# A pooling branch folded into the output projection of a one-core encoder block

## The chip, the cores and the metric

The kernel runs on one core of one Trainium2 chip. The metric is device time in microseconds, the median of several runs. Engines are called by their names here: TensorE (PE in rows) multiplies matrices, VectorE (DVE), ScalarE (ACT) and GpSimd (POOL) work element by element, and SyncE (SP) issues most of the DMA transfers; ScalarE issues some of them too.

## What is computed

One layer of an encoder on 2048 tokens of width 1024, in float32:

```python
h = rms_norm(x, norm1_g)
q, k, v, p = split(h @ w_in)                    # 512, 128, 128, 512 columns
a = sliding_window_sink_attention(rms_norm(q), rms_norm(k), v, sinks)
# pooling, four groups g of 128 channels, windows w = 2, 4, 8, 16
mixed = trailing_mean(p[g], w) - p[g]
m[g]  = (mixed @ pool_w[g] + pool_b[g]) * pool_scale[g]
x = x + concat([a, m]) @ w_out                  # w_out is 1024 x 1024
x = x + conv_glu(rms_norm(x, norm2_g), w_up, conv_w, conv_b, w_down)
```

The pooling map is linear and is followed by a linear projection. So `m @ w_out[512:]` is `mixed` times the product of `pool_w`, the scale and the lower half of `w_out`, plus a constant row that depends on `pool_b`.

## The kernel before

Each float32 operand of TensorE is split in a high and a low half (type fp32r in the rows), and each product is three passes (`passes`, lines 808 to 812: high by high, low by high, high by low). ScalarE makes the high half of a weight tile (`w_hi`), VectorE the low half (`w_lo`), from rows that a DMA brings to one of two `raw` slots. The ring of split weights has three slots, and a unit's halves are made when the unit two places ahead of it is reached (`split(n + LEAD)`).

The tokens go in four blocks a = 0 to 3 of 512. A block has "units", each with one weight tile of 128x1024: four `pin` (p of a pooling group), two `kv`, four `q` and eight `o` (the output projection; the name o(a, h, k) holds the half h of the columns and k of the rows of `w_out`). A unit has 24 products of 128x512, about the same for kv in 48 of 128x256. Units of block 0 are split and their halves are stored to `wA_d` in DRAM, so that later blocks only load them; o units are split anew each time.

What happens when is written out by hand in `attention_order`. Each engine walks that one list and does its own part of every entry, in that order, waiting on semaphores. An engine that waits lets all that stands behind it wait too. These entries matter here:

- `win(a, g)`: VectorE forms the trailing mean less the token in `pbuf`, and then `mix_hi` and `mix_lo` from it.
- `pm(a, g)`: TensorE multiplies these by `pool_w[g]` (`pw_hi`, `pw_lo`), ScalarE evicts with scale and bias (line 1181) into `pbuf`. 16 of them in all.
- `join(a)`: VectorE splits that result into the lower rows of `cat_hi`, `cat_lo`, the left operand of the o units.
- `q(a, 3)`, the last q unit: ScalarE squares each tile (line 1209), VectorE sums (line 1621), GpSimd takes the reciprocal root (lines 2041 and 2043), VectorE scales (line 1626). VectorE does this inside its entry for q(a, 3), so its next weight split, that for o(a-1, 0, 2), stands behind the last scaling.
- `n1sq`, `n1sc`: the squares, roots and scaling of the rows of the next block. `n2sq`, `n2sc`: the same for the second norm. The roots are GpSimd's.
- `inv(a, j)`: GpSimd scales the softmax rows (line 2076).
- `o(a, h, 3)`: VectorE adds the product to the residual rows, `rows[a]`, which a DMA brought from x (line 1615).
- `t2(a, j)`: TensorE transposes the normed rows of block a (line 1033).

Blocks overlap: the o units of block a-1 come after the q units of block a. After the attention part come the up-projection with the convolution and the down-projection (`up`, `load_t`, `load_s`), which the diff does not touch.

Of the kernel before, what the change touches and what calls it, by code (L numbers as in the profile page):

```python
# [5 lines left out]
ALU = mybir.AluOpType  # L6
# [26 lines left out]
RAW, RING, LEAD, MIX = 2, 3, 2, 2  # L33


def attention_order():
# [13 lines left out]
    for a in range(NB):  # L50
        more, back = a + 1 < NB, a > 0
        if a > 1:
            units("kv", a, (0,))
            units("t2", a - 2, (2,))
            units("kv", a, (1,))
            units("kve", a, ())
            units("t2", a - 2, (3,))
        units("q", a, (0,))
        units("pm", a, (0,), (1,))
# [3 lines left out]
        units("q", a, (1,))  # L63
        units("win", a, (3,))
# [3 lines left out]
        units("pm", a, (2,))  # L68
        units("q", a, (3,))
        if back:  # L70
            units("pm", a, (3,))
        else:

            units("t1", a + 1, (0,))
            units("pm", a, (3,))
# [44 lines left out]
        units("inv", a, (1,))  # L120
        if more:
# [49 lines left out]
UNIT_STAGES = ("pin", "kv", "q", "o")  # L171
# [8 lines left out]
SPLIT_NO = {}  # L180
for _n, _s in enumerate(UNITS):
    if _s[1] == 0 or _s[0] == "o":
        SPLIT_NO[_n] = len(SPLIT_NO)
N_SPLIT = len(SPLIT_NO)
KEPT_UNITS = [n for n in SPLIT_NO if UNITS[n][0] != "o"]
# [52 lines left out]
def pm_bank(a, g):  # L238

    return (4, 5, 4, 5 if a == 0 else 7)[g]  # L240
# [84 lines left out]
def bass_hybrid_block(nc, x, norm1_g, w_in, q_norm_g, k_norm_g, attn_sinks, pool_w, pool_b, pool_scale,  # L325
# [15 lines left out]

    with ExitStack() as ctx:
# [32 lines left out]
        def at(name, kib, shape, dt=F32):  # L375
# [8 lines left out]
        mix_hi, mix_lo = at("mix_hi", 68.125, [P, MIX, T], F32R), at("mix_lo", 72.125, [P, MIX, T], F32R)  # L384
        pw_hi, pw_lo = at("pw_hi", 76.125, [P, 4, P], F32R), at("pw_lo", 78.125, [P, 4, P], F32R)
        raw = at("raw", 80.125, [P, RAW, 1024])
# [48 lines left out]
            "mix_ready pool_done m_copied mT_step mT_ready kv_done k_squared k_summed k_step k_rstd k_scaled v_kept "  # L435
# [25 lines left out]
        VECTORS_IN, CONST_IN, CONST_POOL, CONST_STEP, CONST_READY = 7 * 16, 6 * 16, 9, 5, 4  # L461
# [131 lines left out]
        def _(sp):  # L593
            def load(n, src):
                if n in SPLIT_NO:
                    m = SPLIT_NO[n]
                    wait(sp, "split_lo", m - RAW + 1)
                    sp.dma_start(raw[:, m % RAW, :].rearrange("p (k n) -> p k n", k=src.shape[1]), src
                                 ).then_inc(raw_in[m % RAW], 16)
# [27 lines left out]
            def kv(a, n, k):  # L627
# [3 lines left out]
                if k == 1 and a == 1:  # L631
                    sp.wait_ge(S["mix_ready"], 4)
                    sp.wait_ge(const_ready, CONST_READY)
                    sp.dma_start(r[:], x_v[:, 0:NT, :]).then_inc(r_in[0], 16)
# [81 lines left out]
            walk(dict(pin=pin, kv=kv, q=q, o=o, first_loads=first_loads, second_loads=second_loads))  # L716
# [91 lines left out]
        def _(pe):  # L808
# [73 lines left out]
            def pin(a, n, g):  # L882
                halves_there(n)
                if a == 1 and g < 2:

                    pe.wait_ge(S["m_copied"], 3 + g)
# [18 lines left out]
            def pm(a, g):  # L905
                if a == 0 and g == 0:
                    pe.wait_ge(const_ready, CONST_READY)
                pe.wait_ge(S["mix_ready"], 4 * a + g + 1)
                if g < 2:

                    pe.wait_ge(S["p_copied"], 4 * a + g + 1)
                    wait(pe, "h2_copied", KT * (a - 1))
                else:
                    pe.wait_ge(S["m_copied"], 4 * a + g - 1)
                    if pm_bank(a, g) == 7:
                        pe.wait_ge(S["k_scaled"], 2 * a + 2)
                passes(ps[:, pm_bank(a, g), :], pw_hi[:, g, :], pw_lo[:, g, :], mix_hi[:, g % MIX, :],
# [1243 lines left out]
```

## Time and profile before

| | us |
|---|---|
| median of 3 runs | 1776.51 |
| lowest and highest | 1775.22, 1776.84 |
| span of the profiled execution, first to last instruction | 1774.4 |
| TensorE busy | 1755.5 |
| VectorE busy | 1334.7 |
| ScalarE busy | 805.7 |
| GpSimd busy | 247.3 |

No time of the profiled execution apart from its span is given; the span lies 2.1 us under the median of the runs, which also counts what comes ahead of and behind the instructions. Busy time is what the engine spent in instructions; products overlap, so busy TensorE says that it always had one in its pipe. A row of the timeline gives the start, the duration, the engine and line, what was written from what, how many alike are merged (x4), and in brackets the idle time ahead and who ended it.

### The profile page before, as it was taken

What the parts mean: (1) busy time and instruction counts of PE and PEld (TensorE: products, weight loads), DVE (VectorE), ACT (ScalarE), POOL (GpSimd) and SP (SyncE); (2) the same over time, 40 slices, a digit from 0 to 9 for tenths busy, and PEclk for the clock granted to TensorE, in tenths of its full rate; (3) what the DMA queues carried; (4) which work ended last, traced back from release to release, by engine and by line L of the source; (5) the groups of instructions that cost most, each with busy time, mean ns of one, the idle gap of its engine ahead of it and who ended that gap; (6) DMA issues with size and microseconds to landing.
All of it is one profiled execution on the core that took longest, in us unless ns stands there. A gap on an engine that the chain in (4) does not pass through costs nothing.

```text
span 1774.4 us, 23434 instructions
## 1 busy us (share of the span) xinstructions
PE 1755.5 (99%) x8490; PEld 1462.7 (82%) x8490; DVE 1334.7 (75%) x1796; ACT 805.7 (45%) x1437; POOL 247.3 (14%) x270
## 2 busy tenths in 40 slices
PE   7999999999999999999999999999999999999999
PEld 6888888888878888888888888888888888888887
DVE  5645644635779999999998998998998778865774
ACT  4554544534765444444454444444444433333321
POOL 1213212202110000000000000000004033310210
PEclk9999999999999999999999999999999999999999
DMA  8553383484445523323376223223227999976884
GB/s 324 225 220 107 114 311 110 166 290 160 164 171 186 194 84 128 133 83 95 119 251 211 72 83 96 71 84 95 72 83 235 343 343 332 314 254 211 302 286 130
DMA packets 211555, 321.73 MB, mean 181 GB/s; under 512 B 13737, under 2 KB 106097, under 8 KB 211441
## 3 DMA queue, kind: packets, MB, share of 16 engines
q1 hardware_dynamic: 192014, 267.75, 45.3%
q10 hardware_dynamic: 19427, 52.49, 7.6%
q8 instruction: 68, 1.11, 0.3%
q14 instruction: 46, 0.38, 0.1%
HBM read 249.93 MB, written 70.25 MB: 180 GB/s over the span
## 4 chain that ended last, share of the span: by engine, by line
PE 92%; DVE 3%; DMA 2%; ACT 2%; issue 1%; POOL 0%; ACTq 0%; DVEq 0%; POOLq 0%
PE ps L810 29%; PE ps L811 29%; PE ps L812 29%; PE ps L969 1%; PE ps L993 1%; PE ps L980 1%; PE ps L1033 1%; DMA raw<-in_w_out_dram 1%; DMA raw<-in_w_in_dram 1%; DMA gT_d<-cb 0%; DVE hT_lo L1564 0%; DVE va_lo L1788 0%; DVE w_lo L1517 0%; POOL ss_q L2043 0%; PE ps L956 0%
## 5 line engine op out<-in xcount | busy, mean ns | idle before, releaser
L810 PE MATMUL ps<-va_hi,wv 128*128 128x512 f32 x1232 | 479.8, 389 | 1.4 <-DVE va_lo L1751 0.6
L811 PE MATMUL ps<-va_lo,wv 128*128 128x512 f32 x1232 | 479.3, 389 | 0.0
L812 PE MATMUL ps<-va_hi,wv 128*128 128x512 f32 x1232 | 479.3, 389 | 0.0
L810 PEld LDWEIGHTS ps<-va_hi,wv 128*128 128x128 f32 x1232 | 231.3, 188 | 51.3 <-issue 2.8
L812 PEld LDWEIGHTS ps<-va_hi,wv 128*128 128x128 f32 x1232 | 231.3, 188 | 48.0
L811 PEld LDWEIGHTS ps<-va_lo,wv 128*128 128x128 f32 x1232 | 231.3, 188 | 47.6
L810 PE MATMUL ps<-dt_hi,ds_hi 128*128 128x512 f32 x616 | 239.6, 389 | 0.0
L812 PE MATMUL ps<-dt_hi,ds_lo 128*128 128x512 f32 x616 | 239.6, 389 | 0.0
L811 PE MATMUL ps<-dt_lo,ds_hi 128*128 128x512 f32 x616 | 239.6, 389 | 0.0
L1838 DVE SCALAR_TENSOR_TENSOR cb<-ub,cst,cb 128x1024 f32<-128x1024 f32 x176 | 219.8, 1291 | 10.1 <-ACT cb L1357 10.1
L1357 ACT ACTIVATE cb<-ub,cst 128x1024 f32<-128x1024 f32 x88 | 108.9, 1243 | 142.7 <-DVE ub L1893 86.3
L1471 ACT ACTIVATE ds_hi<-dts 128x512 fp32r<-128x512 f32 x110 | 69.5, 632 | 147.7 <-PE ps L812 102.0
L810 PEld LDWEIGHTS ps<-dt_hi,ds_hi 128*128 128x128 f32 x616 | 115.6, 188 | 24.2 <-DVE ds_lo L1998 0.2
L811 PEld LDWEIGHTS ps<-dt_lo,ds_hi 128*128 128x128 f32 x616 | 115.6, 188 | 24.0
L812 PEld LDWEIGHTS ps<-dt_hi,ds_lo 128*128 128x128 f32 x616 | 115.6, 188 | 23.9
L1309 ACT ACTIVATE wv<-tt 128x512 fp32r<-128x512 f32 x168 | 100.3, 623 | 64.9 <-PE ps L812 37.9
L1309 ACT ACTIVATE wv<-rw 128x512 fp32r<-128x512 f32 x126 | 78.4, 624 | 110.2 <-DVE cb L1848 96.3
L2129 POOL TENSOR_TENSOR dtw<-dw 128x512 f32<-128x512 f32 x55 | 90.3, 1642 | 273.4 <-DMA dw<-in_w_down_dram 249.9
L1998 DVE TENSOR_TENSOR ds_lo<-dts,ds_hi 128x512 fp32r<-128x512 f32 x110 | 89.3, 812 | 38.9 <-ACT ds_hi L1471 38.9
L1745 DVE TENSOR_TENSOR wv<-tt,wv 128x512 fp32r<-128x512 f32 x168 | 111.5, 684 | 0.0
L1517 DVE TENSOR_TENSOR w_lo<-raw,w_hi 128x1024 fp32r<-128x1024 f32 x42 | 56.0, 1339 | 72.0 <-ACT w_hi L1109 72.0
L810 PE MATMUL ps<-w_hi,cat_hi 128*128 128x512 f32 x256 | 101.4, 396 | 0.1
(170 smaller groups left out, 2819.7 us busy)
## 6 DMA issues: line engine op xcount, KB each, us to landing
dg<-gT_d SPq DMA_DIRECT2D x264, 256.0 KB, 5.5
rw<-in_w_up_dram SPq DMA_DIRECT2D x84, 512.0 KB, 5.0
dw<-in_w_down_dram SPq DMA_DIRECT2D x132, 256.0 KB, 5.5
gT_d<-cb ACTq DMA_DIRECT2D x44, 512.0 KB, 2.6
raw<-in_w_out_dram SPq DMA_DIRECT2D x32, 512.0 KB, 4.1
w_hi<-wA_d SPq DMA_DIRECT2D x30, 512.0 KB, 3.3
w_lo<-wA_d SPq DMA_DIRECT2D x30, 512.0 KB, 5.2
n<-in_x_dram SPq DMA_DIRECT2D x16, 512.0 KB, 8.2
```

Source lines behind the costliest of these rows:

```text
L810: pe.matmul(out_ap, l_hi, r_hi, start=first, stop=False, skip_group_check=True)
L811: pe.matmul(out_ap, l_hi, r_lo, start=False, stop=False, skip_group_check=True)
L812: return pe.matmul(out_ap, l_lo, r_hi, start=False, stop=last, skip_group_check=True)
L969: mm = pe.matmul(ps[:, S_BANK[t] + v, q], qT[rows, t, q], kT[rows, t, c].rearrange("p a d -> p (a d)"), start=True, stop=True)
L1309: a_.activation(wv_hi[:, wslot(un, i), :], w_source(i), ACT.Copy).then_inc(S["u_hi"], 1)
L1357: a_.activation(cb[:, s, :], ub[:, s, 2:], ACT.Identity, bias=cbias[:, col], scale=cw[2][:, col]).then_inc(S[("tap2g", "tap2v")[s]], 1)
L1471: a_.activation(ds_hi[:, sigma % SSLOTS, :], s_source(sigma), ACT.Copy).then_inc(S["s_hi"], 1)
L1517: v.tensor_tensor(w_lo[:, n % RING, :], raw[:, SPLIT_NO[n] % RAW, :], as_f32(w_hi[:, n % RING, :]), ALU.subtract).then_inc(S["split_lo"], 1)
L1745: v.tensor_tensor(wv_lo[:, w, :], w_source(i), as_f32(wv_hi[:, w, :]), ALU.subtract).then_inc(S["u_lo"], 1)
L1838: v.scalar_tensor_tensor(cb[:, s, :], ub[:, s, j:j + TS], cw[j][:, col], cb[:, s, :], ALU.mult, ALU.add).then_inc(S["conv"], 1)
L1998: v.tensor_tensor(ds_lo[:, sigma % SSLOTS, :], s_source(sigma), as_f32(ds_hi[:, sigma % SSLOTS, :]), ALU.subtract).then_inc(S["s_lo"], 1)
L2129: g_.tensor_tensor(t_source(tau), dw[:, tau % WRAW, 0, :], dw[:, tau % WRAW, 1, :], ALU.subtract if minus else ALU.add).then_inc(S["t_adde ...
```

## The change

The pooling maps no longer work on the tokens. Once, during block 0, the program forms the product of each group's scaled map with its 128 rows of `w_out`, in four new units wp(h, pair) of two groups each, and stores it to DRAM (`wP_d`). The o units with k < 2 then load from there instead of from `w_out`. The sums of `win` go straight to `join`. The bias becomes a row: GpSimd multiplies the raw rows of `w_out` by scale times bias and adds up the groups (`acc`), a product with a matrix of ones sums over the partitions and spreads the row to all of them (`bias`), and GpSimd adds the row to the residual rows of each block (`rb`).

In the hand-written order (all `pm` entries go):

```diff
+        if not back:
+            units("pwt", a, ())
         units("q", a, (0,))
-        units("pm", a, (0,), (1,))
+        if a == 1:
+            units("bias_halves", a, ())
         units("win", a, (2,))
         if more:
             units("n1sq", a + 1, ())
         units("q", a, (1,))
+        if back:
+            units("rb", a - 1, ())
         units("win", a, (3,))
         if more:
             units("n1sc", a + 1, ())
         units("q", a, (2,))
-        units("pm", a, (2,))
+        if a == 1:
+            units("bias", a, ())
+        if not back:
+            units("wp", a, (0, 0))
         units("q", a, (3,))
...
             units("t1", a + 1, (0,))
-            units("pm", a, (3,))
+            units("wp", a, (0, 1))
             units("t1", a + 1, (1,))
...
             units("av", a, (0,), (1,))
+            units("wp", a, (1, 0))
             units("sp", a, (2,), (3,))
             units("pt", a, (2,), (3,))
             units("kv", a + 1, (1,))
             units("av", a, (2,), (3,))
+            units("wp", a, (1, 1))
...
         units("inv", a, (1,))
+        if not more:
+            units("rb", a, ())
```

SyncE's loads:

```diff
                     wait(sp, "split_lo", m - RAW + 1)
+                    if m - RAW in WP_NO:
+                        sp.wait_ge(S["bias_step"], (3, 7, 10, 14)[WP_NO[m - RAW]])
...
+            def wp(a, n, h, pair):
+                load(n, w_out_v[:, 4 + 2 * pair:6 + 2 * pair, h * 512:(h + 1) * 512])
+
             def o(a, n, h, k):
-                kt = (4 + 2 * k) % KT
-                load(n, w_out_v[:, kt:kt + 2, h * 512:(h + 1) * 512])
+                cols = slice(h * 512, (h + 1) * 512)
+                if k < 2:
+                    if a == 0:
+                        sp.wait_ge(S["fold_out"], 16 * KEEP * (h + 1))
+                    load(n, wP_d[:, 2 * k:2 * k + 2, cols])
+                else:
+                    load(n, w_out_v[:, 2 * k - 4:2 * k - 2, cols])
```

TensorE:

```diff
+            def pwt(a):
+                pe.wait_ge(const_in, CONST_IN)
+                pe.wait_ge(S["p_copied"], 1)
+                for g in range(4):
+                    mm = pe.transpose(ps[:, 4, tokens(g)], pw_in[:, g, :], ident[:])
+                mm.then_inc(S["fold_mm"], 1)
...
+                for k in range(2):
+                    g = 2 * pair + k
+                    wait(pe, "fold_copied", 2 * (u - 1) + k + 1)
+                    mm = passes(ps[:, 4 + k, :], pw_hi[:, g, :], pw_lo[:, g, :], hi[:, k, :], lo[:, k, :], True, True)
```

ScalarE and VectorE (the two mix halves of `win` go, and so does the eviction of `pm`):

```diff
+            def wp(a, n, h, pair):
+                u = folded(h, pair)
+                split(n + LEAD)
...
+                    a_.activation(wp_kept[:, i % KEEP, :], ps[:, 4 + k, :], ACT.Copy).then_inc(S["fold_copied"], 1)
...
+                    act.dma_start(wP_d[:, 2 * pair + k, h * 512:(h + 1) * 512], wp_kept[:, i % KEEP, :]
+                                  ).then_inc(S["fold_out"], 16)
...
+            def bias(a):
+                act.wait_ge(S["fold_mm"], 6)
+                a_.activation(bias_all[:], ps[:, 4:6, :], ACT.Copy).then_inc(S["fold_copied"], 1)
...
-                wait(dve, "pool_done", 4 * a + g - MIX + 1)
-                dve.wait_ge(S["win_step"], step)
-                v.tensor_copy(mix_hi[:, g % MIX, :], p_g[:, CARRY:]).then_inc(S["win_step"], 1)
...
-                if h == 0:
-                    dve.wait_ge(r_in[a % 2], 16 * (a // 2 + 1))
                 for t in range(NT):
+                    if h == 0:
+                        dve.wait_ge(S["r_ready"], NT * a + t + 1)
```

GpSimd:

```diff
+            def wp(a, n, h, pair):
+                m = SPLIT_NO[n]
+                pool.wait_ge(const_ready, CONST_READY)
+                pool.wait_ge(S["split_lo"], m + 1)
+                for k in range(2):
+                    g, step = 2 * pair + k, 7 * h + max(0, 4 * pair + 2 * k - 1)
+                    w_g = raw[:, m % RAW, k * T:(k + 1) * T]
+                    into = acc[:, h, :] if g == 0 else w_g
+                    wait(pool, "bias_step", step)
+                    g_.tensor_tensor(into, w_g, pbias[:, g:g + 1].broadcast_to([P, T]), ALU.mult).then_inc(S["bias_step"], 1)
+                    if g > 0:
+                        pool.wait_ge(S["bias_step"], step + 1)
+                        g_.tensor_tensor(acc[:, h, :], acc[:, h, :], w_g, ALU.add).then_inc(S["bias_step"], 1)
+
+            def rb(a):
+                if a == 0:
+                    pool.wait_ge(S["fold_copied"], BIAS_COPIED)
+                pool.wait_ge(r_in[a % 2], 16 * (a // 2 + 1))
+                for t in range(NT):
+                    g_.tensor_tensor(rows[a][:, t, :], rows[a][:, t, :], bias_all[:].rearrange("p h n -> p (h n)"), ALU.add
+                                     ).then_inc(S["r_ready"], 1)
```

GpSimd in block 1 before, from the last root of the next block's norm to the first roots of q(1,3):

```order
L2041 TENSOR_SCALAR rstd<-ss 128x1 [waits sq1]
L2043 TENSOR_TENSOR rstd<-rstd,half_neg 128x1 [waits step1]
L2041 TENSOR_SCALAR ss_q<-ss_q 128x8 [waits q_summed]
L2043 TENSOR_TENSOR ss_q<-ss_q,half_neg 128x8 [waits q_step]
L2041 TENSOR_SCALAR ss_q<-ss_q 128x8 [waits q_summed]
```

And GpSimd at the same place after the change, where L2181 is the add of `rb`:

```order
L2120 TENSOR_SCALAR rstd<-ss 128x1 [waits sq1]
L2122 TENSOR_TENSOR rstd<-rstd,half_neg 128x1 [waits step1]
L2181 TENSOR_TENSOR r<-r,bias_all 128x1024 [waits r_in0,fold_copied]
L2181 TENSOR_TENSOR r<-r,bias_all 128x1024 x3
L2120 TENSOR_SCALAR ss_q<-ss_q 128x8 [waits q_summed]
L2122 TENSOR_TENSOR ss_q<-ss_q,half_neg 128x8 [waits q_step]
```

The four adds stand ahead of the roots of q, and the first of them waits for the evicted bias row (fold_copied).

TensorE in block 1 before, from the end of q(1,2) to the start of q(1,3), with the product pm(1,2) between them:

```order
L812 MATMUL ps<-w_hi,hT_lo 128x512
L810 MATMUL ps<-mix_hi,pw_hi 128x512 [waits m_copied,mix_ready]
L811 MATMUL ps<-mix_lo,pw_hi 128x512
L812 MATMUL ps<-mix_hi,pw_lo 128x512
L810 MATMUL ps<-w_hi,hT_hi 128x512 [waits dw_in1]
```

TensorE at that place after the change:

```order
L842 MATMUL ps<-w_hi,hT_lo 128x512
L961 MATMUL ps<-acc_hi,ones 128x512 [waits fold_copied,fold_lo]
L962 MATMUL ps<-acc_lo,ones 128x512
L961 MATMUL ps<-acc_hi,ones 128x512
L962 MATMUL ps<-acc_lo,ones 128x512
L840 MATMUL ps<-w_hi,hT_hi 128x512 [waits dw_in2]
```

The three passes of pm(1,2) are gone and the four bias products stand in their place, right ahead of q(1,3).

GpSimd at the end of the attention after the change, from the softmax scaling of block 3 (L2155) to the roots of the second norm of block 2 (before, these two stood next to each other):

```order
L2155 TENSOR_TENSOR xs<-xs,row_sum 128x1024 [waits inv_ready] x4
L2181 TENSOR_TENSOR r<-r,bias_all 128x1024 [waits r_in1]
L2181 TENSOR_TENSOR r<-r,bias_all 128x1024 x3
L2120 TENSOR_SCALAR rstd<-ss 128x1 [waits sq2]
L2122 TENSOR_TENSOR rstd<-rstd,half_neg 128x1 [waits step2]
```

Here too four adds have moved in ahead of roots that VectorE's scaling (n2sc) waits for.

## Rows read from the trace of the kernel before

**Rows 1.** The page: span, and busy time of each engine.

```profile
span 1774.4 us, 23434 instructions
PE 1755.5 (99%) x8490; PEld 1462.7 (82%) x8490; DVE 1334.7 (75%) x1796; ACT 805.7 (45%) x1437; POOL 247.3 (14%) x270
```

**Rows 2.** TensorE's timeline, start of q(1,3) to start of o(0,0,2).

```profile
148.60 0.39 PE L810 MATMUL ps<-w_hi,hT_hi 128*128 128x512 f32 x1
...
165.61 0.60 PE L946 MATMUL ps<-ident,xs 128*128 128x128 f32 x4
165.96 0.48 PE L810 MATMUL ps<-w_hi,cat_hi 128*128 128x512 f32 x1
```

**Rows 3.** TensorE's timeline behind the two attention mixings of block 0.

```profile
119.90 0.52 PE L980 MATMUL ps<-ident,xs 128*128 128x128 f32 x3 [0.64 <-DVE cat_lo L1720]
...
130.12 0.47 PE L810 MATMUL ps<-w_hi,hT_hi 128*128 128x512 f32 x1 [0.64 <-DVE cat_lo L1720]
```

**Rows 4.** Timelines of TensorE, ScalarE and VectorE in block 0.

```profile
49.96 0.40 PE L810 MATMUL ps<-w_hi,hT_hi 128*128 128x512 f32 x1
...
56.31 1.46 ACT L1181 ACTIVATE pbuf<-ps,pbias,cst 128x512 f32<-128x512 f32 x2 [3.77 <-PE ps L812]
...
63.51 1.23 DVE L1517 TENSOR_TENSOR w_lo<-raw,w_hi 128x1024 fp32r<-128x1024 f32 x1 [4.21 <-ACT w_hi L1109]
...
68.60 0.43 DVE L1592 CAST mix_hi<-pbuf 128x512 fp32r<-128x512 f32 x1
...
69.67 2.74 DVE L1528 TENSOR_SCALAR n<-n,rstd 128x1024 f32<-128x1024 f32 x4
```

**Rows 5.** pin(1,0): its load's issue, its first product; page 6, landing.

```profile
62.42 0.32 SPq L613 DMA_DIRECT2D w_hi<-wA_d  x1
...
76.49 0.48 PE L810 MATMUL ps<-hT_hi,w_hi 128*128 128x512 f32 x1
...
w_lo<-wA_d SPq DMA_DIRECT2D x30, 512.0 KB, 5.2
```

**Rows 6.** GpSimd by tile: duration ns min/median/max, first and last start.

```profile
L2076 POOL TENSOR_TENSOR xs<-xs,row_sum x16: 1895/1898/2879, 101.5 to 456.6; 128x1024 f32<-128x1024 f32 x16
...
L2129 POOL TENSOR_TENSOR dtw<-dw x55: 1284/1540/4072, 1339.2 to 1701.4; 128x512 f32<-128x512 f32 x55
```

**Rows 7.** ScalarE's timeline, two evictions of 128x1024.

```profile
110.78 1.94 ACT L1242 ACTIVATE PT<-ps 128x1024 f32<-128x1024 f32 x2
```

**Rows 8.** GpSimd's timeline, first and last of the four roots of q(1,3).

```profile
152.47 0.20 POOL L2041 TENSOR_SCALAR ss_q<-ss_q 128x8 f32<-128x8 f32 x1 [7.11 <-DVE ss_q L1621]
...
158.77 1.64 POOL L2043 TENSOR_TENSOR ss_q<-ss_q,half_neg 128x8 f32<-128x8 f32 x1
```

**Rows 9.** VectorE's timeline behind them.

```profile
160.44 0.69 DVE L1626 TENSOR_TENSOR xs<-ps,ss_q 128x512 f32<-128x512 f32 x1 [1.31 <-POOL ss_q L2043]
161.05 2.35 DVE L1517 TENSOR_TENSOR w_lo<-raw,w_hi 128x1024 fp32r<-128x1024 f32 x2
```

**Rows 10.** Block 2: start of q(2,0), issue of its residual rows, and their landing.

```profile
253.55 0.48 PE L810 MATMUL ps<-w_hi,hT_hi 128*128 128x512 f32 x1
...
255.93 0.51 ACTq L1293 DMA_DIRECT2D r<-in_x_dram  x1
...
r<-in_x_dram ACTq DMA_DIRECT2D x1, 2048.0 KB, 13.1
```

**Rows 11.** GpSimd's timeline at the end of the attention.

```profile
454.73 3.75 POOL L2076 TENSOR_TENSOR xs<-xs,row_sum 128x1024 f32<-128x1024 f32 x2 [12.27 <-DVE row_sum L1690]
458.57 0.19 POOL L2041 TENSOR_SCALAR rstd<-ss 128x1 f32<-128x1 f32 x1
...
462.54 0.55 POOL L2043 TENSOR_TENSOR rstd<-rstd,half_neg 128x1 f32<-128x1 f32 x1
```

**Rows 12.** VectorE and TensorE there.

```profile
470.53 0.69 DVE L1720 TENSOR_TENSOR cat_lo<-ps,cat_hi 128x512 fp32r<-128x512 f32 x1 [3.77 <-ACT cat_hi L1249]
...
471.28 0.55 PE L1033 MATMUL ps<-ident,n 128*128 128x128 f32 x3 [0.51 <-DVE cat_lo L1720]
```

More of the change, by code:

```diff
@@ L67, in attention_order @@
         units("q", a, (2,))
-        units("pm", a, (2,))
+        if a == 1:
+            units("bias", a, ())
+        if not back:
+            units("wp", a, (0, 0))
         units("q", a, (3,))
-        if back:
-            units("pm", a, (3,))
-        else:
+        if not back:
             units("t1", a + 1, (0,))
-            units("pm", a, (3,))
+            units("wp", a, (0, 1))
             units("t1", a + 1, (1,))
@@ L170 @@
 ORDER = attention_order()
-UNIT_STAGES = ("pin", "kv", "q", "o")
+UNIT_STAGES = ("pin", "kv", "q", "wp", "o")
 UNIT = {}
@@ L180 @@
 SPLIT_NO = {}
+WP_NO = {}
 for _n, _s in enumerate(UNITS):
     if _s[1] == 0 or _s[0] == "o":
+        if _s[0] == "wp":
+            WP_NO[len(SPLIT_NO)] = len(WP_NO)
         SPLIT_NO[_n] = len(SPLIT_NO)
 N_SPLIT = len(SPLIT_NO)
-KEPT_UNITS = [n for n in SPLIT_NO if UNITS[n][0] != "o"]
+KEPT_UNITS = [n for n in SPLIT_NO if UNITS[n][0] not in ("wp", "o")]
 def first_unit(n):
@@ L714, in second_loads @@
                     load_vs(1, j)
-            walk(dict(pin=pin, kv=kv, q=q, o=o, first_loads=first_loads, second_loads=second_loads))
+            walk(dict(pin=pin, kv=kv, q=q, wp=wp, o=o, first_loads=first_loads, second_loads=second_loads))
             wait(sp, "v_lo", V_DONE[1, 4])
@@ L903, in pin @@
                 mm.then_inc(S["unit_used"], 1)
[L905 to L917, printed above, removed]
-                       mix_lo[:, g % MIX, :], True, True).then_inc(S["pool_done"], 1)
+            def pwt(a):
[6 more added lines that the diff above has]
+                u = folded(h, pair)
+                halves_there(n)
+                pe.wait_ge(S["fold_lo"], 4)
+                pe.wait_ge(S["p_copied"], (2, 2, 6, 6)[u])
+                hi = w_hi[:, n % RING, :].rearrange("p (k n) -> p k n", k=2)
+                lo = w_lo[:, n % RING, :].rearrange("p (k n) -> p k n", k=2)
+                for k in range(2):
+                    g = 2 * pair + k
+                    wait(pe, "fold_copied", 2 * (u - 1) + k + 1)
+                    mm = passes(ps[:, 4 + k, :], pw_hi[:, g, :], pw_lo[:, g, :], hi[:, k, :], lo[:, k, :], True, True)
+                    if k == 0:
+                        mm.then_inc(S["fold_mm"], 1)
+                mm.then_inc(S["unit_used"], 1)
+            def bias(a):
+                pe.wait_ge(S["fold_lo"], BIAS_FOLDED)
+                pe.wait_ge(S["fold_copied"], 8)
+                for h in range(2):
+                    pe.matmul(ps[:, 4 + h, :], ones[:], acc_hi[:, h, :], start=True, stop=False, skip_group_check=True)
+                    mm = pe.matmul(ps[:, 4 + h, :], ones[:], acc_lo[:, h, :], start=False, stop=True, skip_group_check=True)
+                mm.then_inc(S["fold_mm"], 1)
             def h_left(i, t):
@@ L1036, in _ @@
             pe.wait_ge(const_pool, CONST_POOL)
-            walk(dict(t1=t1, pin=pin, pm=pm, kv=kv, q=q, kt=kt, qt=qt, s=s, sp=sp, av=av, o=o, t2=t2))
+            walk(dict(t1=t1, pin=pin, pwt=pwt, wp=wp, bias=bias, kv=kv, q=q, kt=kt, qt=qt, s=s, sp=sp, av=av, o=o, t2=t2))
             def up(un):
@@ L1342, in va3 @@
                 v_hi(1, 3)
-            walk(dict(n1=n1_, n1sq=n1sq, t1=t1, pin=pin, pc=pc, pm=pm, kv=kv, kve=kve, q=q, kt=kt, qt=qt, s=s, pt=pt, av=av,
+            walk(dict(n1=n1_, n1sq=n1sq, t1=t1, pin=pin, pc=pc, pwt=pwt, wp=wp, bias_halves=bias_halves, bias=bias, kv=kv, kve=kve, q=q, kt=kt, qt=qt, s=s, pt=pt, av=av,
                       o=o, n2sq=n2sq, t2=t2, first_weights=first_weights, va=va, va3=va3))
@@ L1572, in win @@
                 dve.wait_ge(S["p_copied"], 4 * a + g + 1)
-                step, p_g = 18 * a + STEP0[g], pbuf[:, g, :]
+                step, p_g = 10 * a + STEP0[g], pbuf[:, g, :]
+                wait(dve, "mix_ready", 4 * a + g)
                 src, lag = p_g, 1
@@ L2097, in _ @@
             g_.memset(half_neg[:], -0.5).then_inc(const_pool, 1)
+            g_.memset(as_f32(ones[:]), 1.0).then_inc(const_pool, 1)
             for ap in (k_keep[:], v_even[:], p_keep[:], halo[:]):
```

90 lines of the change are left out of this document (60 added, 30 removed).

## The prediction

> **What bounds the kernel now.** I read the page first: TensorE is busy for 1755.5 of the 1774.4 us of the span, VectorE for 75% of it, GpSimd for 14% [rows 1]. So a microsecond of TensorE work removed anywhere is a microsecond of time, and a microsecond in which another engine makes TensorE wait is one too. The second thing to read is what a matrix product costs. Its row says 0.39 us, but that is its latency. The timeline gives the spacing: from 148.60 to 165.61 us there are 75 products of 128x512 (24 of q(1,3), 3 of the old pm, 48 of two o units), 17.01 us, so 0.227 us each; four transposes take 0.35 us (165.61 to 165.96) [rows 2]. Then I looked for idle gaps of TensorE around the edits. Two of 0.64 us stand in the first block, each behind the attention mixing, where the next unit waits for cat_lo [rows 3].
>
> **TensorE's own work.** Removed: 16 pooling products of three passes, 48 products. Added: 24 for the folding, 4 for the bias row, and 4 transposes. Net 20 fewer, 20 x 0.227 = 4.5 us, less 0.4 us of transposes [rows 2]: **-4.1 us**. The two gaps: wp(1,0) and wp(1,1) (1.36 us each) are put exactly there, and need no cat_lo, so each 0.64 us wait is filled: **-1.3 us** [rows 3]. Together -5.4 us.
>
> **Where VectorE and ScalarE are relieved.** 32 casts and subtracts of the mix halves and 16 evictions go, against 4 more split units, 8 evictions and 8 stores. Neither engine sets the end there: TensorE had no other idle time at those places. I cost this at nothing; its cover is the long queue of TensorE units.
>
> **The first block.** VectorE now makes q(0,3)'s low half behind the scaling of the next block's rows, because wp(0,0) has moved ahead of it. Before, ScalarE stood idle 3.77 us for the pooling product and spent 1.46 us on evicting it; without both (1.36 of the latter is on the path), and with some 1.3 us of new evictions of the scaled maps (an estimate from the 128x512 rows), its chain is 3.8 us earlier, so VectorE's split at 63.51 comes at 59.7 [rows 4]. Behind it: split 1.15, window sums 3.95 (63.51 + 1.15 to 68.60, where the mix halves began), scaling 2.75, split 1.15: ready at 68.7 [rows 4]. TensorE comes there at 49.96 + 0.4 + 72 x 0.227 + 6 x 0.227 = 68.1. **+0.6 us**; bounds 0 (if one of those runs faster) and 1.5 (if ScalarE's copies and stores between t1's evictions push the paced stretch after 76 us as well). Behind it in SyncE's queue: the load of wp(0,1)'s rows now waits for GpSimd's three bias products (bias_step), and the load of pin(1,0)'s weights is queued behind it and behind q(0,3)'s stores. Before, that load was issued at 62.42; now it can't be before wp(0,0) is used and q(0,3)'s low half is made, 68.7, and four issues (62.42 to some 64 for two) bring it to about 70; its second half takes 5.2 us in the median, 75.4, and pin(1,0) begins at 76.49 [rows 5]. Cost 0, with 1 us to spare.
>
> **The residual rows, the part that decides.** Each block now has four adds of 128x1024 on GpSimd, in order with the reciprocal roots that VectorE waits for. What does one cost? The nearest rows are the scaling of the probabilities, 128x1024 with one operand broadcast, 1.90 us at least, and the sum of two full 128x512 operands, 1.28 us at least and 1.54 in the median, while VectorE is busy [rows 6]. Doubling the second gives 2.57 (fixed part counted twice) and 3.08 (contended). Bounds 1.9 and 3.1; I take D = 2.4, below the doubled minimum, since the form (two full operands) is that of the second row and the fixed part is not paid twice. Four take 9.6 us.
>
> The Trainium skill (GPSIMD Engine Reference, 3.1 Elementwise) gives 4497 ns for an fp32 add of 2048 elements on GpSimd, so an estimate by that page is 2.25 us here; it also calls about 2.6 cycles an element the floor for two inputs, which speaks against the 1.90 row as a price. By 2.25 the stalls below would be 3.3, 1.1 and 1.6 us and the sum +1.2 us, 1777.7, instead of +3.0. The page's section 8 says that this engine is about half as fast as VectorE elementwise; no run here shows the same add on both.
>
> *Block 1.* Let Q be the start of q(1,3), 148.60 before [rows 2]. rb(0) waits for the evicted bias row, and the bias products stand right before q(1,3). Eviction of 128x1024 takes 1.0 us (1.94 for two) [rows 7], so GpSimd starts at Q+1.3 and is done at Q+1.3+4D. Only then do the four roots for q come: 152.47 to 160.41, 7.9 us [rows 8]. VectorE stands in its own order behind them: last root, last scaling, then the split for o(0,0,2), 160.41 to 162.2, 1.8 us [rows 8, 9]. Ready at Q+11.0+4D. TensorE wants it after q(1,3), two o units and four transposes: 72 x 0.227 + 0.35 = Q+16.7. Stall 4D - 5.7 = **+3.9 us** (1.9 to 6.7). Before, the same split was ready at Q+13.6, with some 3.8 us to spare; now nothing but that spare covers 9.6 us.
>
> *Block 2.* rb(1) waits for no bias, but for its residual rows. Their load is issued 2.4 us after q(2,0) starts (255.93 against S = 253.55) and lands 13.1 us later [rows 10]: S+15.5. The rest is the same: S+15.5+4D+7.9+1.8, against a use at S+16.4+16.7 (72 products and a switch, then as above). Stall 4D - 7.9 = **+1.7 us** (0 to 4.5).
>
> *Block 3.* rb(2) waits for no bias and no roots of a next block, and its rows are asked for at kv(3,1). Three q units, 16.3 us, lie between the roots of k and q(3,3), against 9.6: 0.
>
> *The end of the attention.* rb(3) stands between the probability scaling, done at 458.5, and the roots of the second norm. Those took until 463.09, 4.6 us with one slow one, 4.0 without, and now end at 458.5 + 4D + 4.0 [rows 11]; VectorE's last scaling 0.75, then cat_lo 0.65, which transposes t2(2,0) wait for: 463.9+4D against 471.28 before [rows 12]. **+2.2 us** (0.2 to 5.0).
>
> **Sum.** -5.4 + 0.6 + 3.9 + 1.7 + 2.2 = +3.0 us; GpSimd's memset of ones ends before its first root, which waits for ScalarE. The profiled execution's span is 1774.4; the runs' median is 1776.5, 2.1 us around the span, so **1779.5 us**.
>
> **Rivals.**
> *Hidden adds.* If GpSimd's 9.6 us never reach TensorE, only -5.4 + 0.6 is left: 1771.7 us, faster. For it speaks that GpSimd is busy 14% [rows 1]; against it, that this share is an average and that VectorE's queue goes through these roots before it splits the next weights. It decides if VectorE's stall ends before Q+16.7, that is D below 1.4. No row is that cheap for two full operands.
> *Cheap adds.* D = 1.9, as the scaling row: -4.8 + 1.9 + 0 + 0.2 = -2.7, 1773.8 us, no measurable change.
> *Contention.* GpSimd's sums are 20% slower in the median than at best while VectorE works [rows 6]. With D = 3.1: -4.8 + 6.7 + 4.5 + 5.0 = +11.4, 1787.9 us, slower. VectorE mostly waits during these adds, which speaks against it; a half-way case (D = 2.7) gives +6.6, 1783. From D of about 2.46 on the change is slower measurably.
> *The queue in the first block.* SyncE waits for GpSimd's bias_step before wp(0,1)'s load, and pin(1,0)'s weights are queued behind. If these take 7 to 9 us to land instead of 5.2, as other loads behind 2 MB of traffic do (13.1 for r) [rows 5, 10], pin(1,0) waits 1 to 3 us on top: 1780.5 to 1782.5, slower. It decides from a landing of 6.3 us on.
>
> **How the numbers follow.** Within 0.2% (3.6 us) of 1776.5 is what a measurement of this kernel can't tell from no change. Stalls at D of 2.2 to 2.6, 0.52: times 1777 to 1782, two thirds of it inside the 0.2% (0.33) and a third above (0.19). Contention or the queue, 0.21, slower. Cheap adds, 0.12, same. Hidden adds or a gain I don't see, 0.15, faster. So faster 0.15, same 0.45, slower 0.40. The likeliest case's own range is 1777 to 1782. The range leaves out most of the hidden case and the top of contention: 1773 to 1786.
>
> **What the profile after would show.** TensorE with 20 fewer 128x512 products; the two 0.64 us gaps gone; idle before o(0,0,2) of about 4 us, released by VectorE's w_lo; the same of 1 to 2 us before o(1,0,2), none before o(2,0,2); 2 to 3 us before the transposes of t2(2,0), released by cat_lo; GpSimd's four adds at 2.4 us. I am wrong if the adds cost far from 2.4, if r's rows land later or earlier in block 2, or if a wait shows up in the first block that the raw slots or ScalarE's stores make.

## The result, and the profile after

The changed kernel takes 1793.8 us (median of 4 runs, 1790.5 to 1795.4), beside 1776.7 for the kernel before on the same chip: a ratio of 1.0098, 95% interval 1.0086 to 1.0109, slower by 17.1 us. The forecast was 1779.5, range 1773 to 1786: the time lies outside it. The profiled execution has a span of 1793.6 us, 19.2 more than before, and a mean granted clock of 0.994.

The page says almost nothing of this. TensorE's busy time answers to [rows 1]:

```profile
span 1793.6 us, 23457 instructions
...
PE 1759.2 (98%) x8474; PEld 1465.2 (82%) x8474; DVE 1348.4 (75%) x1771; ACT 804.8 (45%) x1439; POOL 306.4 (17%) x301
```

There are 16 instructions fewer than before (20 products less, 4 transposes more), and yet 3.7 us *more* busy time. That is the first hint that some of them ran slower. The view of waits of the changed kernel's TensorE (us in total, times, longest) says where it stood idle:

```profile
PE ps L840 <- DVE w_lo L1592: 11.2, 3, 5.4
...
PE ps L1079 <- DVE cat_lo L1801: 5.7, 1, 5.7
```

The three waits for w_lo are at q(0,3), 2.29 us, at o(0,0,2), 5.41, and at o(1,0,2), 3.46; the one for cat_lo is at t2(2,0), 5.72. These are the four places of the forecast, and o(2,0,2) has none, as forecast; the two gaps of 0.64 us [rows 3] are gone. The forecast gave the four places 0.6, 3.9, 1.7 and 2.2 us more than before: 8.4 together. They measure 16.9, or 16.4 more than before, since TensorE waited 0.51 us at t2(2,0) in the kernel before too [rows 12].

Windows laid around the four waits, TensorE alone (busy time and count, granted clock, DMA share, GB/s), show a second cost:

```profile
62.00:68.00 6.00, 6.00 (x27) 1.00 0.24 79
68.00:70.30 2.30, 0.01 (x2) 0.93 0.07 25
70.30:74.00 3.70, 3.70 (x10) 0.58 0.82 324
74.00:78.00 4.00, 4.00 (x23) 1.00 0.99 335
164.00:169.90 5.90, 5.90 (x29) 1.00 0.00 0
169.90:175.30 5.40, 0.03 (x1) 0.73 0.00 0
175.30:179.00 3.70, 3.65 (x9) 0.50 0.56 194
179.00:183.00 4.00, 4.00 (x20) 0.98 0.28 90
298.20:301.50 3.30, 0.00 (x0) 1.00 0.00 0
301.50:305.00 3.50, 3.46 (x9) 0.58 0.61 199
305.00:309.00 4.00, 4.00 (x19) 0.94 0.37 96
481.80:487.40 5.60, 0.00 (x0) 0.91 0.01 1
487.40:492.00 4.60, 4.51 (x15) 0.50 0.02 4
492.00:497.00 5.00, 5.00 (x23) 0.88 0.44 150
```

Read each place downwards: nothing done (the clock falls to 0.50 during the wait or within 0.6 us of its end), then 3.5 to 4.6 us at a mean granted clock of 0.50 to 0.58, where 0.50 is 1.2 GHz instead of 2.4, then back towards full clock. Product by product (timeline of TensorE, start and duration):

```profile
175.35 0.77 PE L840 MATMUL ps<-w_hi,cat_hi 128*128 128x512 f32 x1 [5.41 <-DVE w_lo L1592]
175.91 0.63 PE L841 MATMUL ps<-w_lo,cat_hi 128*128 128x512 f32 x1
176.34 0.63 PE L842 MATMUL ps<-w_hi,cat_lo 128*128 128x512 f32 x1
176.76 0.63 PE L840 MATMUL ps<-w_hi,cat_hi 128*128 128x512 f32 x1
...
179.27 0.39 PE L840 MATMUL ps<-w_hi,cat_hi 128*128 128x512 f32 x1
```

The starts are 0.43 us apart instead of the 0.227 of [rows 2]. (The Trainium skill, TensorE: Matmul & The Clock Gate, Part 1, has 426.7 ns from start to start at the lower clock for 512 columns; the trace agrees.) The unit of 24 products takes 7.36 us at o(0,0,2), 7.15 at o(1,0,2), 7.03 at q(0,3). After a short wait, at full clock, it takes 5.57, as the second run with extra products below shows (175.44 to 181.01). That makes 1.8, 1.6 and 1.5 us. At the end of the attention, eight transposes and 24 products take 9.12 us (487.49 to 496.61) instead of 6.42, as the run with adds of half the size shows (468.27 to 474.69): 2.7. So the books of the two profiled executions nearly close: 16.4 us of idle time more than before, 7.6 of slow products, -5.4 forecast for TensorE's own work and the filled gaps, +18.6 of the +19.2 us. This is one execution, the slowest of the four (1795.4 us). In other traces below, a wait of the same length at the end of the attention is followed by a shorter slow stretch.

Why are the waits twice as long? GpSimd's adds, which have no row before (timeline, POOL; each row is four adds):

```profile
154.32 10.99 POOL L2181 TENSOR_TENSOR r<-r,bias_all 128x1024 f32<-128x1024 f32 x4 [4.16 <-ACT bias_all L1257]
...
280.06 11.43 POOL L2181 TENSOR_TENSOR r<-r,bias_all 128x1024 f32<-128x1024 f32 x4 [4.96 <-DMA r<-in_x_dram]
...
469.52 11.43 POOL L2181 TENSOR_TENSOR r<-r,bias_all 128x1024 f32<-128x1024 f32 x4
```

Four take 11.0 to 11.4 us, not 9.6. One by one (the same view with narrow windows), those that run by themselves take 2.36 to 2.41 us, and those beside one of VectorE's low halves 2.94 to 3.44; the low halves are stretched too, where one takes 1.22 us alone (GpSimd's adds of r by tile, with minimum, median and maximum in ns, then VectorE's timeline; its second row is two low halves):

```profile
L2181 POOL TENSOR_TENSOR r<-r,bias_all x12: 2356/2672/3445, 154.3 to 478.6; 128x1024 f32<-128x1024 f32 x12
...
155.22 3.12 DVE L1592 TENSOR_TENSOR w_lo<-raw,w_hi 128x1024 fp32r<-128x1024 f32 x1 [0.22 <-ACT w_hi L1155]
...
282.76 6.48 DVE L1592 TENSOR_TENSOR w_lo<-raw,w_hi 128x1024 fp32r<-128x1024 f32 x2 [5.71 <-ACT w_hi L1155]
```

The groups of four start where the forecast put them: 1.3 us after q(1,3) starts at 153.01, and 15.4 after q(2,0) starts at 264.70. And in the first block, GpSimd and VectorE of the changed kernel side by side (timeline):

```profile
60.43 1.38 POOL L2171 TENSOR_TENSOR acc<-raw,pbias 128x512 f32<-128x512 f32 x1 [0.92 <-DVE w_lo L1592]
61.88 1.38 POOL L2171 TENSOR_TENSOR raw<-raw,pbias 128x512 f32<-128x512 f32 x1
63.34 1.63 POOL L2174 TENSOR_TENSOR acc<-acc,raw 128x512 f32<-128x512 f32 x1
...
60.94 4.59 DVE L1654 TENSOR_TENSOR sums<-sums 128x525 f32<-128x525 f32 x3
...
66.38 2.73 DVE L1603 TENSOR_SCALAR n<-n,rstd 128x1024 f32<-128x1024 f32 x4
69.03 2.35 DVE L1592 TENSOR_TENSOR w_lo<-raw,w_hi 128x1024 fp32r<-128x1024 f32 x2
```

Three window sums run beside GpSimd's three instructions, two products and a sum, and each ends 0.55 to 0.57 us behind one of them. They take 4.59 us; by themselves they take 2.17, as the run with everything off GpSimd shows. Behind them come the scaling and the low half of q(0,3).

### The profile page after: what moved, and what is told of

It is laid out like the page before. It is cut to its first block, busy times and chain, and to the rows that moved or that the text cites. A ratio compares the mean times of both kernels' runs of the same rounds, so it can differ in the third digit from the quotient of the medians.

```text
span 1793.6 us, 23457 instructions
## 1 busy us (share of the span) xinstructions
PE 1759.2 (98%) x8474; PEld 1465.2 (82%) x8474; DVE 1348.4 (75%) x1771; ACT 804.8 (45%) x1439; POOL 306.4 (17%) x301
## 4 chain that ended last, share of the span: by engine, by line
PE 88%; POOL 4%; DVE 4%; ACT 2%; DMA 1%; issue 1%; ACTq 0%; DVEq 0%; POOLq 0%
PE ps L840 28%; PE ps L842 28%; PE ps L841 28%; POOL r L2181 2%; POOL ss_q L2122 1%; ACT xs L1306 1%; DVE w_lo L1592 1%; DMA r<-in_x_dram 1%; PE ps L1079 1%; PE ps L1038 1%; PE ps L1025 1%; PE ps L1014 1%; DMA gT_d<-cb 0%; DVE va_lo L1867 0%; PE ps L1001 0%
## 5 line engine op out<-in xcount | busy, mean ns | idle before, releaser
L1592 DVE TENSOR_TENSOR w_lo<-raw,w_hi 128x1024 fp32r<-128x1024 f32 x46 | 67.6, 1480 | 59.0 <-ACT w_hi L1155 59.0
```

The lines of the kernel that those rows point to most:

```text
L1592: v.tensor_tensor(w_lo[:, n % RING, :], raw[:, SPLIT_NO[n] % RAW, :], as_f32(w_hi[:, n % RING, :]), ALU.subtract).then_inc(S["split_lo"], 1)
```

## The experiments

**Theory:** (1) the adds and bias products on GpSimd make VectorE late, by their place in GpSimd's order and by holding back VectorE's instructions that run beside them; (2) each wait of TensorE that follows costs its length and, through the granted clock, some 1.5 to 2.7 us more (measured in the one trace above). **Rivals:** the clock falls for a reason of its own; the waits come of the folding's work as such. The ratio behind each time is to the kernel before, timed beside it (1776.0 to 1776.1 us there). Comments in the diffs are mine, and "..." stands for lines left out.

**Adds behind the roots.** Only the order on GpSimd is changed:

```diff
         units("q", a, (1,))
-        if back:
-            units("rb", a - 1, ())
...
         units("q", a, (3,))
+        if back:
+            units("rb", a - 1, ())
...
         units("inv", a, (1,))
-        if not more:
-            units("rb", a, ())               # a = 3
...
     units("n2sq", last - 1, ())
+    units("rb", last, ())
```

> The changed kernel, with GpSimd's four adds of the bias row placed behind the reciprocal roots that they delayed: rb(0), rb(1), rb(2) behind the roots of q (after q(1,3), q(2,3), q(3,3)), rb(3) behind the second norm's roots. Theory (the adds stand in order ahead of roots, VectorE's low halves come late, TensorE idles and then works at a lower granted clock): the idle times of 5.41, 3.46 and 5.72 us go, and with them 1.8 + 1.6 + 2.2 us of slow products, 20.2 us together: 1773.6 us (1771 to 1776), and TensorE's granted clock is 1.00 at those places. Rival A (the clock falls for a reason of its own): only 14.6 us go, 1779.2, and the clock is still below 1.0 there. Rival B (the adds then run beside VectorE's splits and slow them, so that new waits for w_lo appear behind o(0,0,2)): 1777 to 1782.

Measured: 1781.2 us (ratio 1.0027, 1.0017 to 1.0037), 12.6 less than the changed kernel. Both waits for w_lo in blocks 1 and 2 are gone and the clock is 1.00 there, so rival A is out. But 5.2 us of wait stay at the end of the attention. Its cause, GpSimd and VectorE of this kernel (timeline):

```profile
462.05 11.59 POOL L2180 TENSOR_TENSOR r<-r,bias_all 128x1024 f32<-128x1024 f32 x4
...
463.07 11.12 DVE L1602 TENSOR_SCALAR n<-n,rstd 128x1024 f32<-128x1024 f32 x4
474.11 1.28 DVE L1800 TENSOR_TENSOR cat_lo<-ps,cat_hi 128x512 fp32r<-128x512 f32 x2
```

VectorE's four scalings of one operand, 2.73 us by themselves (the same form in the changed kernel at 66.38), take 11.12: one for each add. The total fits rival B, contention, at a place that it did not name: behind o(0,0,2) there was slack enough. (The Trainium skill, SBUF — State Buffer, "Who interferes with whom", calls the port pair of the two engines an exclusive lock, which the one holds for its whole instruction while the other is blocked. These rows agree.) Not every instruction of VectorE is held. One with an operand in PSUM isn't: the scaling of q's last tile (L1706, xs<-ps,ss_q), at 165.69, runs beside the first add, which starts at 165.62, and takes 0.69 us as ever. Neither is a sum along the rows of one operand: in the changed kernel two of 128x512 take 1.26 us beside an add (L1702, at 158.27), and 1.27 here with GpSimd's adds out of the way (at 156.95).

**wp(0,0) behind q(0,3)**, in the order of all engines, the rest as in the changed kernel:

```diff
-            units("wp", a, (0, 0))
         units("q", a, (3,))
+        if not back:
+            units("wp", a, (0, 0))
```

> The changed kernel, with only wp(0,0) moved from ahead of q(0,3) to behind it in the order of all engines, so that q(0,3)'s low half is made ahead of the window sums and the scaling of the next rows, as in the kernel before. Theory (the 2.29 us wait before q(0,3) comes of that order, and the slow products behind it of the wait): 2.29 + 1.57 = 3.9 us less, 1789.9 us (1789 to 1791). Rival (the stretch is late by VectorE's and ScalarE's total work, so the wait moves to wp(0,0) or t1(1,0)): within 1 us of 1793.8.

Measured: 1794.8 us (1.0104, 1.0090 to 1.0117); the rival. The 2.29 us are gone; in their place stand these (waits of TensorE):

```profile
PE ps L1014 <- ACT xs L1306: 2.8, 2, 1.7
...
PE ps L909 <- DMA w_lo<-wA_d: 1.7, 1, 1.7
```

The second is the queue rival of the prediction: the load of pin(1,0)'s stored low half. In the changed kernel TensorE came there 4 us later (79.88 instead of 76.01) and it was hidden. The first is contention again: the join's eight conversions (4 casts, 4 subtractions) take 9.9 us beside GpSimd's bias products and their sums, from 89.15 to 99.05, where they take 3.8 in the kernel before, and the scores' exponentials are late.

**Both moves.**

> Both moves at once: the adds behind the roots and wp(0,0) behind q(0,3). If the four waits are independent and are all that the change costs, TensorE's own saving is left, with the two filled gaps: 1776.5 - 4.1 - 1.3 = 1771.1, by the sums of the two theories 1793.8 - 20.2 - 3.9 = 1769.7; so 1770 to 1772, faster than the kernel before by 0.3 to 0.4%. Rival (contention of GpSimd's adds with VectorE): 1774 to 1779.

Measured: 1782.1 us (1.0033, 1.0022 to 1.0044), not told from the adds' move alone, and far from my 1770 to 1772. It has 2.9 us for the exponentials, 1.9 for the stored low half, and 4.9 for cat_lo at the end: moved beside other work of VectorE, GpSimd's work costs there about what it cost before.

**Extra products in the wait.** TensorE multiplies something nobody reads; nothing else is moved:

```diff
+                    for i in range((18, 9, 0, 0)[a]):     # in o(a,0,2), behind kt
+                        if i == 0:
+                            pe.wait_ge(S["kT_ready"], a + 2)
+                        pe.matmul(ps[:, 0, :], hT_hi[:, i % KT, 0:P], hT_hi[:, i % KT, :], start=True, stop=True)
```

> The changed kernel, with extra matrix products whose result nobody reads (18 of 128x512 ahead of o(0,0,2) in block 1 and 9 ahead of o(1,0,2) in block 2), so that TensorE works during most of the waits of 5.41 and 3.46 us; nothing else is moved, the low halves come as late as before. Theory (it is the idle time that makes the granted clock fall): o(0,0,2) and o(1,0,2) start when they did, 175.4 and 301.5, but the clock stays near 1.00 behind them, and 1.8 + 1.6 us go: 1790.4 (1789.5 to 1791.5). Rival A (the products behind the wait are slow by something that comes with the late operands, or the clock falls on its own): 1793.8, no change. Rival B (extra products lie on the path): 1794 to 1800.

Measured: 1794.4 us (1.0100, 1.0086 to 1.0114). Not an answer: the extra products had to wait 2.04 us for kT themselves, in block 1 the clock fell within 0.6 us of that wait's end, and 18 of them took 5.9 us instead of 4.1, which pushed o(0,0,2) from 175.35 to 178.0. In block 2 the extra products waited 2.04 us as well, and there the clock stayed at 1.00. So they were put ahead of kt, where nothing is waited for:

```diff
+                for i in range((0, 18, 9, 0)[a]):         # in kt(a), ahead of its transposes
+                    pe.matmul(ps[:, 0, :], hT_hi[:, i % KT, 0:P], hT_hi[:, i % KT, :], start=True, stop=True)
```

> The changed kernel, with extra matrix products whose result nobody reads ahead of the transposes kt (18 of 128x512 in block 1, 9 in block 2), where TensorE has no wait before them; so that it stands idle for about 1.3 us instead of 5.41 ahead of o(0,0,2), and 1.4 instead of 3.46 ahead of o(1,0,2). The low halves come as late as before: these two units start at 175.4 and 301.5. Theory (a long idle time of TensorE is what the granted clock falls after): no product behind them is slow, and 1.8 + 1.6 us go, 1790.4 (1789.5 to 1791.5). Rival (any wait makes it fall, or it falls at these places on its own): 1793.8, clock about 0.74 over the unit o(0,0,2) as in the changed kernel.

Measured: 1790.4 us (1.0081, 1.0067 to 1.0094), 3.4 less with 27 products *more*. The unit o(0,0,2) starts at 175.44, after 1.28 us of idle time, on the same late low half, and takes 5.57 us instead of 7.36. The unit o(1,0,2) starts 2.4 us earlier than in the changed kernel, at 299.13 after 0.69 us of idle time, and also takes 5.57, instead of 7.15. Windows of TensorE, of the changed kernel and of this one:

```profile
175.00:183.00 8.00, 7.65 (x27) 0.74 0.40 135
```

```profile
175.00:183.00 8.00, 7.56 (x42) 1.00 0.45 137
```

So it is the idle time that the clock falls after, and the slow products are a price of their own. That the total meets the theory's 3.4 us to a tenth is luck. The two profiled executions differ by 5.0 us: 3.4 at these two units, and 1.3 at the end of the attention, where the same wait (5.67 us, 5.72 before) is followed by 7.8 us for eight transposes and 24 products instead of 9.12. Nothing there was changed. So the price behind one and the same wait varies from trace to trace, here between 1.4 and 2.7 us.

**The adds on VectorE**, in the gaps of its order:

```diff
+            RB_AT = (((0,), (1,), (2,), (3,)), ((0, 1), (2, 3), (), ()))
...
                 if k < 3:
                     split(n + LEAD)
+                    for t in RB_AT[a + 1 == NB][k] if h == 0 else ():
+                        rb(a, t)           # the same add as GpSimd's, on VectorE
```

> The changed kernel, with the sixteen adds of the bias row on VectorE instead of GpSimd: one behind each low half in the units o(a,0,k), for the last block two behind each of its first two. GpSimd keeps only the folding's bias products. Theory (GpSimd's adds cost by their place in its order and by holding back VectorE's instructions that run beside them; on VectorE one costs 1.22 us and neither happens): the waits of 5.41, 3.46 and 5.72 us and their slow products go, also the one that the adds behind the roots left at the end of the attention (5.18 us and slow products): 1781.2 - 7.4 = 1773.8 (1772 to 1776). Rival (16 adds of 1.22 us in VectorE's order push its low halves or evictions late, with new waits of TensorE behind o(a,0,2) and before o(a,1,0)): 1777 to 1783.

Measured: 1774.4 us (0.9990, 0.9981 to 0.9998). The adds are 1.22 us each here, less than half of GpSimd's (one tile's rows: minimum, median and maximum in ns):

```profile
L1690 DVE TENSOR_TENSOR r<-r,bias_all x12: 1216/1218/1220, 165.9 to 464.8; 128x1024 f32<-128x1024 f32 x12
```

TensorE waits for w_lo only at q(0,3), 2.3 us, 0.7 for pin(1,0)'s stored low half and 1.3 for cat_lo at the end, and in this trace the clock falls behind none of them. This one edit gives back 19.4 us.

**The first block's window sums later**, alone, the rest as in the changed kernel:

```diff
-        units("win", a, (3,))
+        if back:
+            units("win", a, (3,))
         if more:
             units("n1sc", a + 1, ())
         units("q", a, (2,))
+        if not back:                         # a = 0
+            units("win", a, (3,))
```

> The changed kernel, with only the window sums of group 3 of the first block moved on VectorE from ahead of the scaling and q(0,3)'s low half to behind them. Theory (the 2.29 us wait before q(0,3) is the window sums' 5.4 us, of which 2.4 us come of running beside GpSimd's bias products): the wait and its slow products go, 3.9 us: 1789.9 (1789 to 1791). Rival (as with wp(0,0) moved: TensorE is earlier, and the wait is met further on, since GpSimd's next bias products slow VectorE's join and the exponentials come late): 1792 to 1794.5.

Measured: 1789.6 us (1.0074, 1.0061 to 1.0087), 4.2 less: the theory. Its trace has no wait for w_lo and no slow product there, and a new wait of 0.6 us for pin(1,0)'s stored low half.

**Everything off GpSimd**: the two edits above, and the bias products as multiply-adds on VectorE behind each folding unit's low half:

```diff
+                if UNITS[n][0] == "wp":           # in VectorE's split(n)
...
+                            v.scalar_tensor_tensor(acc[:, h, :], w_g, b_g, acc[:, h, :], ALU.mult, ALU.add
+                                                   ).then_inc(S["bias_step"], 1)
```

> All together: the adds on VectorE, the bias products of the folding on VectorE too (8 multiply-adds of 128x512 instead of GpSimd's 8 products and 6 adds), and the window sums of group 3 behind q(0,3)'s low half. Then GpSimd does nothing that the kernel before doesn't do. If the stalls, their slow products and the contention are all that the change costs, TensorE's own saving is left: 1776.5 - 4.1 - 1.3 = 1771.1, or 1793.8 - 20.2 - 3.9 = 1769.7; so 1769 to 1772, faster than the kernel before. Rival (the folding's extra work on VectorE and ScalarE in the first block leaves waits of 2 to 4 us there, as the moved wp(0,0) showed): 1772 to 1776, no measurable change.

Measured: **1771.4 us** (0.9975, 0.9964 to 0.9985), faster than the kernel before. The granted clock is 1.00 throughout. Apart from the one at the very start, none of TensorE's waits in the attention is longer than 1.1 us; of those that grew, the longest is 1.0 us for cat_lo at the end, 0.5 before. VectorE's window sums, now with GpSimd idle beside them, are in the second fence:

```profile
PE ps L839 <- DVE hT_lo L1650: 2.7, 5, 1.1
PE ps L1078 <- DVE cat_lo L1826: 1.0, 1, 1.0
```

```profile
66.24 2.17 DVE L1665 TENSOR_TENSOR sums<-sums 128x525 f32<-128x525 f32 x3
```

**The bias products back on GpSimd**, the rest as in the last one.

> The adds of the rows on VectorE and the window sums of group 3 behind q(0,3)'s low half, but the folding's bias products still on GpSimd (the fastest kernel so far, 1771.4, with this one part put back). Theory (the bias products cost only where they run beside VectorE's instructions: its window sums, now with nobody waiting, and its join): 0.6 us of wait for pin(1,0)'s stored low half and up to 1.2 us at pin(1,3) come back, as in the run with the window sums moved alone: 1772.9 (1772 to 1774). Rival (they cost nothing now): 1771.4. Second rival (join comes late and the scores wait as they did with wp(0,0) moved, 2.8 us): 1774.5.

Measured: 1772.2 us (0.9977, 0.9968 to 0.9986), between theory and rival and not told from the 1771.4. In this kernel and the last the folding's own work is all still there, so the long waits didn't come of it as such. The trace has the wait for pin(1,0)'s stored half, at 1.3 us, and waits for cat_lo and va_lo that are 0.3 and 0.4 us longer. The 1.2 us at pin(1,3) don't come back, and I had misread them: in the run with the window sums moved alone, a wait of that length (1.17 us, for p_keep) stands at 38.52 us, in block 0 and ahead of what that edit moves.

**Adds of half the size on GpSimd**, behind the roots:

```diff
-                    g_.tensor_tensor(rows[a][:, t, :], rows[a][:, t, :], bias_all[:].rearrange("p h n -> p (h n)"), ALU.add
-                                     ).then_inc(S["r_ready"], 1)
+                    for h in range(2):
+                        y = rows[a][:, t, h * T:(h + 1) * T]
+                        add = g_.tensor_tensor(y, y, bias_all[:, h, :], ALU.add)
+                    add.then_inc(S["r_ready"], 1)
```

> The kernel with the adds behind the roots, each GpSimd add of 128x1024 cut into two of 128x512; the same sums, twice as many instructions. There VectorE's four scalings of 128x1024 took 11.1 us beside four adds of 2.9 us, where they take 2.7 us alone, and left TensorE 5.18 us of wait at the end of the attention. Theory (one VectorE instruction gets through per GpSimd instruction, as long as GpSimd has instructions to run): the four scalings take about 4 x 1.4 = 5.7 us, cat_lo comes some 5 us earlier, that wait is 0 to 0.5 us and the slow products behind it go: 1781.2 - 5 - 2 = 1774 (1772.5 to 1776). The low halves that took 3.1 us each beside adds in block 1 take 1.5 to 1.7. Rival (VectorE gets a share of the time, whatever the instructions' size): the scalings still take 11 us and the time stays at 1781.

Measured: 1778.0 us (1.0015, 1.0006 to 1.0024). VectorE of this kernel, and one row of ScalarE (timeline):

```profile
460.78 6.84 DVE L1602 TENSOR_SCALAR n<-n,rstd 128x1024 f32<-128x1024 f32 x4
467.54 1.27 DVE L1800 TENSOR_TENSOR cat_lo<-ps,cat_hi 128x512 fp32r<-128x512 f32 x2
468.74 2.34 DVE L1879 TENSOR_TENSOR tt<-rw 128x1024 f32<-128x1024 f32 x1
471.11 1.67 DVE L1886 TENSOR_TENSOR tt<-rw,tt 128x512 f32<-128x512 f32 x1
472.81 1.66 DVE L1891 TENSOR_TENSOR tt<-rw,tt 128x512 f32<-128x512 f32 x1
...
474.00 0.63 ACT L1383 ACTIVATE wv<-rw 128x512 fp32r<-128x512 f32 x1 [6.05 <-POOL r L2182]
...
480.52 1.23 DVE L1591 TENSOR_TENSOR w_lo<-raw,w_hi 128x1024 fp32r<-128x1024 f32 x1 [1.55 <-ACT w_hi L1154]
```

The scalings fall from 11.1 to 6.8 us: again one for each GpSimd instruction, now of 1.7 us. So the hold goes by the instruction, as the theory had it (with 1.4 each, though), and the wait for cat_lo fell from 5.2 to 1.0. The low halves in block 1 come out longer than the theory's 1.5 to 1.7: two take 3.92 us, a third 1.56. I missed the total, 1774, for two reasons that stand in these rows. The hold goes on: the differences for the first weights of the up-projection take 2.34, 1.67 and 1.66 us instead of 1.22, 0.69 and 0.69. And ScalarE waits 6.05 us for the last of GpSimd's adds, because the change has it wait for all of them (`act.wait_ge(S["r_ready"], NT * NB)`) ahead of these weights; with the adds on VectorE it starts there at 468.56 without a wait. Both lead to VectorE's split at 480.52, which waits for ScalarE's w_hi, and behind it TensorE waits 2.7 us for an eviction of VectorE's, until 486.0, with the clock at 0.69 from 486 to 496. How the two share that wait isn't shown. (ScalarE's wait for the last add is there in the run with the adds behind the roots too, at 3.4 us, beside the longer wait for cat_lo.)

## Why the prediction was wrong, step by step

- **"A microsecond in which another engine makes TensorE wait is one too"** failed, and it isn't in any term of the sum. Each of the four waits cost 1.5 to 2.7 us on top by the granted clock, 7.6 us in all in the profiled execution; filling two of them took 3.4 us off the two units behind them, the first of which started on its low half as late as ever. Without it no value of D in the range of bounds would have closed the books.
- **D = 2.4, "below the doubled minimum"** was mis-sized: it measured 2.36 at least, 2.67 in the median and 3.45 at most, 2.75 to 2.86 over a group of four. For an add with nothing of VectorE's beside it, 2.4 was right (2.36 to 2.41); what a chain of four costs is the contended figure. The argument "VectorE mostly waits during these adds" was the wrong one: it makes low halves in blocks 1 and 2 just then, and one or two instructions suffice (in block 2 two of them took 6.48 us together instead of 2.35, and GpSimd's adds were stretched with them).
- **The formulas of the waits held.** With the measured adds, block 1 gives 10.99 - 5.7 = 5.3 (measured 5.41), block 2 gives 11.43 - 7.9 = 3.5 (3.46), block 3 zero (none). The end gives 11.43 - 7.4 = 4.0, and 5.0 with roots that took 5.0 us instead of 4.0; it measured 5.72, which is 5.2 more than the 0.51 of before, and the formula counts from there.
- **First block, "+0.6, bounds 0 and 1.5"**: the chain was the right one, but its window sums were priced from a trace in which GpSimd stood idle beside them. 2.4 us more, and the wait is 2.29. I had priced GpSimd's new products only as something SyncE waits for.
- **TensorE's own work and the filled gaps, -5.4**: right. With everything off GpSimd, TensorE is busy for 1751.4 us, 4.1 less than before. With the stalls out, the best version is 4.6 us under the kernel before, and waits 0.5 us longer than it for cat_lo at the end.
- **The rivals.** Contention, with D = 3.1 and 1787.9 us, named the direction and came nearest, with half of its mechanism: GpSimd slowed by VectorE. That half made the waits of blocks 1, 2 and the end 1.4 to 1.8 us longer each, by the formulas. The other half, VectorE held by GpSimd, made the wait in the first block, and the 5.2 us that stayed when the adds were moved behind the roots. The queue rival was absent in the changed kernel and showed itself (0.6 to 1.9 us) as soon as the first wait was shortened.

## What to carry to other kernels

Before moving work to an idle GpSimd, list what VectorE does in the same microseconds: each of its scalings, casts, low halves and sums of two operands in SBUF may last as long as GpSimd's instruction beside it (a scaling's 0.75 us became 2.84 here), and GpSimd's instruction is stretched in turn, so a share of 14% busy is no measure of room. Price a wait of a saturated TensorE at its length plus the slow stretch behind it; when one can't be avoided, moving TensorE's work into it should be worth more than its own time (here only unused products were put there). And the same 16 adds were cheap on the busier engine: 19.5 us of VectorE's time at 1.22 each, hidden, against 45 us of GpSimd's at the head of a queue. Last, look for every instruction that waits for the moved work: here ScalarE's wait for the last add showed only when the longer wait beside it was shortened.

## What was not expected of the hardware

GpSimd and VectorE, both with instructions ready, took turns one for one: four scalings for four adds, and with the adds behind the roots two low halves in 6.12 us instead of 2.35, while the adds beside them took up to 3.4 instead of 2.4. And a wait of the same length didn't always make the clock fall. The 2.27 to 2.29 us before q(0,3) were followed by products 0.43 us apart in the traces of the changed kernel, of the adds behind the roots and of both with extra products, but by full speed in those of the adds on VectorE and of the half adds. The 2.04 us ahead of the extra products made it fall in block 1 and not in block 2. Waits of 1.1 and 1.7 us close behind each other, for the exponentials, made it fall with both moves (0.50 from 106.3 on) and not with wp(0,0) moved alone. What decides between them stays open; single waits up to 1.3 us had no slow stretch behind them in any trace read here.
